# Two more products of the second block moved forward at each layer's start, in a three-layer fp32 transformer kernel

## What is computed

```
mod = silu(c) @ ada_w[i] + ada_b[i];  shift, scale, gate = split(mod, 3)
h   = rms_norm(x, norm_g[i]) * (1 + scale) + shift
proj = h @ w_in                       # the stage that the change touches
out = mixer(proj) @ w_out             # retention, banded attention, latent attention
x   = x + gate * out
```

## Time and profile before

| | us |
|---|---|
| time, median of 3 runs | 2511.5 (2510.46 to 2511.74) |
| the profiled execution, its own time | 2513.0 |
| its span, first to last instruction | 2511.1 |
| TensorE busy | 2455.8 |
| VectorE busy | 1620.3 |
| GpSimd busy | 1221.9 |
| ScalarE busy | 1111.1 |

### The profile page before, as it was taken

How to read it: one execution, slowest core, us unless ns; L and a number is a source line. 1 busy time by engine, 2 the same in 40 slices (tenths; PEclk the granted TensorE clock), 3 DMA queues, 4 the chain that set the end, 5 groups by cost and what they waited for, 6 DMA issues and landing times.

```text
span 2511.1 us, 38631 instructions
## 1 busy us (share of the span) xinstructions
PE 2455.8 (98%) x15068; PEld 2154.1 (86%) x15068; DVE 1620.3 (65%) x2189; ACT 1111.1 (44%) x2060; POOL 1221.9 (49%) x873
## 2 busy tenths in 40 slices
PE   6999999999999999999999999999999999899999
PEld 5888898865588899999998899999988888688887
DVE  6966656487533399795876335666434679888864
ACT  4322223334444342222223336777534434788861
POOL 1545545430044455554455445565454455566664
PEclk9999999999999999999999999999999999999999
DMA  6454544484034334442333357454134353200034
GB/s 261 147 177 140 191 143 165 153 312 138 27 109 157 110 132 151 165 147 93 110 109 118 109 156 208 133 156 117 61 122 159 105 171 98 91 1 1 1 119 158
DMA packets 239472, 327.89 MB, mean 131 GB/s; under 512 B 19246, under 2 KB 172078, under 8 KB 237500
## 3 DMA queue, kind: packets, MB, share of 16 engines
q1 hardware_dynamic: 237820, 325.32, 39.1%
q10 hardware_dynamic: 1472, 0.10, 0.0%
HBM read 246.06 MB, written 79.33 MB: 130 GB/s over the span
## 4 chain that ended last, share of the span: by engine, by line
PE 87%; DVE 8%; issue 2%; ACT 1%; DMA 1%; SPq 0%; POOL 0%; DVEq 0%; ACTq 0%
PE ps L1042 22%; PE ps L1044 22%; PE ps L1043 22%; PE ps L1345 4%; PE ps L1485 2%; PE ps L1333 2%; PE ps L1467 2%; PE ps L1261 2%; PE ps L1280 2%; DVE s_raw L2056 1%; PE ps L1274 1%; PE ps L1185 1%; DVE s_lo L2043 1%; PE ps L1056 1%; DVE raw L2073 1%
## 5 line engine op out<-in xcount | busy, mean ns | idle before, releaser
L932 POOL TENSOR_TENSOR w_lo<-raw,w_hi 128x512 fp32r<-128x512 f32 (+1 forms) x570 | 825.6, 1456 | 1006.7 <-ACT w_hi L1567 1006.0
L1567 ACT ACTIVATE w_hi<-raw 128x512 fp32r<-128x512 f32 (+1 forms) x574 | 355.4, 628 | 1008.5 <-PE ps L1044 796.7
L1042 PE MATMUL ps<-w_hi,s_hi 128*128 128x256 f32 (+1 forms) x1088 | 308.6, 284 | 1.6 <-DVE s_lo L2043 1.3
L1043 PE MATMUL ps<-w_lo,s_hi 128*128 128x256 f32 (+1 forms) x1088 | 307.3, 282 | 0.0
L1044 PE MATMUL ps<-w_hi,s_lo 128*128 128x256 f32 (+1 forms) x1088 | 307.3, 282 | 0.0
L2087 DVE TENSOR_TENSOR u<-u,ps 128x1024 f32<-128x1024 f32 (+1 forms) x128 | 155.3, 1213 | 184.6 <-PE ps L1044 180.2
L1042 PE MATMUL ps<-w_hi,a_hi 128*128 128x256 f32 (+1 forms) x816 | 230.6, 283 | 0.0
L1043 PE MATMUL ps<-w_lo,a_hi 128*128 128x256 f32 (+1 forms) x816 | 230.5, 283 | 0.0
L1044 PE MATMUL ps<-w_hi,a_lo 128*128 128x256 f32 (+1 forms) x816 | 230.5, 282 | 0.0
L2073 DVE TENSOR_TENSOR raw<-raw 128x1024 f32<-128x1024 f32 (+1 forms) x128 | 179.6, 1403 | 60.1 <-DMA raw<-in_w 57.2
L1042 PEld LDWEIGHTS ps<-w_hi,s_hi 128*128 128x128 f32 x1088 | 208.7, 192 | 9.9 <-issue 9.4
(11 more groups left out here) (320 smaller groups left out, 5966.3 us busy)
## 6 DMA issues: line engine op xcount, KB each, us to landing
raw<-in_w SPq DMA_DIRECT2D x191, 512.0 KB, 4.5
ada_c<-in_ada SPq DMA_DIRECT2D x14, 2304.0 KB, 10.4
blk<-u SPq DMA_DIRECT2D x62, 512.0 KB, 3.2
blk<-c SPq DMA_DIRECT2D x31, 512.0 KB, 3.9
blk<-m1s SPq DMA_DIRECT2D x31, 512.0 KB, 3.3
ada_first<-in_ada SPq DMA_DIRECT2D x12, 768.0 KB, 16.3
r_g<-blk SPq DMA_DIRECT2D x8, 1024.0 KB, 9.7
r_v<-blk SPq DMA_DIRECT2D x4, 2048.0 KB, 12.8
```

What stands on the lines that cost most here:

```text
L932: pool.tensor_tensor(w_ring(w_lo, n), w_source(n), w_ring(w_hi, n).bitcast(F32), ALU.subtract)\
L1042: pe.matmul(out, a_hi_, b_hi_, start=first, stop=False, skip_group_check=True)
L1043: pe.matmul(out, a_hi_, b_lo_, start=False, stop=False, skip_group_check=True)
L1567: act.activation(w_ring(w_hi, n), w_source(n), ACT.Copy).then_inc(w_rounded, 1)
```

## The change

Product 0 of the second block moves from third to second place, and product 1 from behind the whole first block to fourth place. Products 0 and 1 of the second block are accumulated in one pair of PSUM banks: ScalarE copies product 0 out (now to a tile of its own, `m1_second`), then product 1 is added on top by TensorE, and `evict(s, "c11")` becomes a copy. Product 1 gets its own weights tile and load. The transposes stay in the second product of the order. The order of VectorE's fourth weight sum in the first block, the bank numbers and the waits on them follow.

```diff
-    start = [(first, 0), (first, 1), second[0]] + [(first, i) for i in range(2, 7)] + second[1:]
+    start = [(first, 0), second[0], (first, 1), second[1]] + [(first, i) for i in range(2, 7)] + second[2:]
...
-        raw_second = place("raw_second", 124, [P, 1024])
+        raw_second = [place(f"raw_second{i}", at, [P, 1024]) for i, at in enumerate((124, 120))]
+        m1_second = [place(f"m1_second{l}", at, [P, 1024]) for l, at in enumerate((186, 186, 196))]
...
             if s in FIRST_BLOCK[0:3]:
-                return (0, 1, 2, 3, 1, 3, 2)[i]
+                return (0, 0, 2, 3, 0, 3, 2)[i]
             if s - 1 in FIRST_BLOCK[0:3]:
-                return (0, 1, 0, 2, 3, 1, 2)[i]
+                return (1, 1, 1, 3, 0, 2, 3)[i]
...
             load_raw(R11, 0)
+            load_second(0, 0)
             load_raw(R21, 0)
...
-            load_second(0)
+            load_second(0, 1)
...
-                        if s == FIRST_BLOCK[l] and i == 1 and k == 1:
+                        if (s, i, k) == (FIRST_BLOCK[l] + 1, 0, 1):
                             turn_half(l, 1, range(4, 8))
...
             def m1s_copy(s):
                 act.wait_ge(w_used, product_end(s, 0))
-                act.wait_ge(stored["c21"], 16 * s)
-                act.activation(quad_tile(m1s, s), product_banks(s, 0), ACT.Copy).then_inc(m1s_done, 1)
+                if s - 1 not in FIRST_BLOCK[0:3]:
+                    act.wait_ge(stored["c21"], 16 * s)
+                act.activation(quad_tile(m1_home(s), s), product_banks(s, 0), ACT.Copy).then_inc(m1s_done, 1)
...
-                hi(PRODUCT[s, 1])
+                hi(PRODUCT[s + 1, 0])
                 if l:
                     stats(l, 1, 3)
-                hi(PRODUCT[s, 1] + 1)
+                hi(PRODUCT[s + 1, 0] + 1)
                 m1s_copy(s)
-                product_slots(s + 1, 0)
+                product_slots(s, 1)
...
-                product_slots(s + 1, 1)
+                product_slots(s + 1, SECOND_ORDER[2])
...
+                if what == "c11" and s - 1 in FIRST_BLOCK[0:3]:
+                    dve.tensor_copy(quad_tile(c11, s), product_banks(s, 1)).then_inc(ev, 1)
+                    return
...
-                for n in range(2 if l else 0, 4):
+                for n in range(2 if l else 0, 3):
                     weight_sum(s, n)
                 variant_low(l, "a22", 0)
                 turned(l, 1, 1)
+                weight_sum(s, 3)
                 variant_low(l, "a22", 1)
                 evict(s, "c11")
```

More of the change, by code:

```diff
@@ L273, in build_program @@
         ld = [sem(f"raw_in{j}") for j in range(5)]
-        second_in = sem("second_in")
+        second_in = [sem(f"second_in{i}") for i in range(2)]
         w_rounded, w_split, w_used = sem("w_rounded"), sem("w_split"), sem("w_used")
@@ L408, in raw_quad, with second_quad, m1_home @@
             return raw[j][:, 0:4 * BLOCKS[s][3]].rearrange("p (k n) -> p k n", k=4)
-        def second_quad(s):
-            return raw_second[:, 0:4 * BLOCKS[s][3]].rearrange("p (k n) -> p k n", k=4)
+        def second_quad(s, i):
+            return raw_second[i][:, 0:4 * BLOCKS[s][3]].rearrange("p (k n) -> p k n", k=4)
+        def m1_home(s):
+            return m1_second[FIRST_BLOCK.index(s - 1)] if s - 1 in FIRST_BLOCK[0:3] else m1s
         def ada_bank(s):
@@ L422, in w_source @@
                 nw = BLOCKS[s][3]
-                if i == 0 and s - 1 in FIRST_BLOCK[0:3]:
-                    return second_quad(s)[:, 2 * j:2 * j + 2]
+                if i < 2 and s - 1 in FIRST_BLOCK[0:3]:
+                    return second_quad(s, i)[:, 2 * j:2 * j + 2]
                 return raw_quad(SOURCE[i], s)[:, 2 * j:2 * j + 2]
@@ L570, in load_raw, with load_second @@
                     .then_inc(ld[j], 16)
-            def load_second(l):
+            def load_second(l, i):
                 s = FIRST_BLOCK[l] + 1
@@ L576, in load_second @@
                     sp.wait_ge(w_used, out_end(l - 1, 3))
-                nw, w0 = BLOCKS[s][3], BLOCKS[s][0]
-                sp.dma_start(second_quad(s), t["w"][w0:w0 + 4, :, 0:nw].rearrange("k p n -> p k n")).then_inc(second_in, 16)
+                nw, w0 = BLOCKS[s][3], BLOCKS[s][0] + 4 * i
+                sp.dma_start(second_quad(s, i), t["w"][w0:w0 + 4, :, 0:nw].rearrange("k p n -> p k n"))\
+                    .then_inc(second_in[i], 16)
             def load_pair(l, p):
@@ L727, in out_loads @@
                 if l < LAST:
-                    load_second(l + 1)
+                    for i in range(2):
+                        load_second(l + 1, i)
                     for b in range(4):
@@ L1064, in bank_wait @@
                         pe.wait_ge(ev, evicted(s - 1, "c12"))
-                    if i < 2 and s > 0:
+                    if i == 0 and s > 0:
                         pe.wait_ge(o_free, 16 * FIRST_BLOCK.index(s) - 4)
+                    if i == 1:
+                        pe.wait_ge(m1s_done, s + 1)
                     if i > 3:
@@ L1070, in bank_wait @@
                 if s - 1 in FIRST_BLOCK[0:3]:
[L1071 to L1076, removed]
+                    if i == 1:
+                        pe.wait_ge(m1s_done, s + 1)
+                    elif i in (3, 4, 5):
+                        pe.wait_ge(ev, evicted(s - 1, {3: "v", 4: "u3", 5: "c12"}[i]))
+                    elif i in (2, 6):
+                        pe.wait_ge(ev, evicted(s, {2: "c11", 6: "u2"}[i]))
                     return
                 if s - 2 in FIRST_BLOCK[0:3] and i < 4:
-                    pe.wait_ge(ev, evicted(s - 1, ("c21", "v", "c12", "u3")[i]))
-                    if i == 3 and s - 1 in ADA_BLOCKS:
+                    pe.wait_ge(ev, evicted(s - 1, ("u3", "c21", "v", "c12")[i]))
+                    if i == 0 and s - 1 in ADA_BLOCKS:
                         pe.wait_ge(m_row, ADA_BLOCKS.index(s - 1) + 1)
@@ L1095, in block_product @@
                 out = product_banks(s, i)
+                added = i == 1 and s - 1 in FIRST_BLOCK[0:3]
                 bank_wait(s, i)
@@ L1104, in block_product @@
                         k = 2 * j + e
-                        if s == FIRST_BLOCK[l] and i == 1 and k == 1:
+                        if (s, i, k) == (FIRST_BLOCK[l] + 1, 0, 1):
                             turn_half(l, 1, range(4, 8))
-                        if s == FIRST_BLOCK[l] and i == 1 and k == 3:
+                        if (s, i, k) == (FIRST_BLOCK[l] + 1, 0, 3):
                             turn_half(l, 1, range(4))
@@ L1114, in block_product @@
                                 mm = product(out[:, b], hi[:, e, cut], lo[:, e, cut], x_hi[v][:, k], x_lo[v][:, k],
-                                             k == 0, k == 3)
+                                             k == 0 and not added, k == 3)
                             else:
                                 mm = product(out[:, b // 2, b % 2], x_hi[v][:, k, cut], x_lo[v][:, k, cut],
-                                             hi[:, e], lo[:, e], k == 0 and b % 2 == 0, k == 3)
+                                             hi[:, e], lo[:, e], k == 0 and b % 2 == 0 and not added, k == 3)
                     mm.then_inc(w_used, 1)
@@ L1546, in hi @@
                     _, s, i, j = kind
-                    if i == 0 and s - 1 in FIRST_BLOCK[0:3]:
+                    if i < 2 and s - 1 in FIRST_BLOCK[0:3]:
                         if j == 0:
-                            act.wait_ge(second_in, 16 * (FIRST_BLOCK.index(s - 1) + 1))
+                            act.wait_ge(second_in[i], 16 * (FIRST_BLOCK.index(s - 1) + 1))
                     elif j == 0 and i in (0, 1, 6):
@@ L1668, in first_block @@
                     turned(l, 1, k)
-                hi(PRODUCT[s, 2])
+                m1s_copy(s + 1)
+                hi(PRODUCT[s + 1, 1])
                 variant(l, "a22", 1)
                 turned(l, 1, 0)
-                hi(PRODUCT[s, 2] + 1)
+                hi(PRODUCT[s + 1, 1] + 1)
                 for k in (2, 3):
                     turned(l, 1, k)
+                product_slots(s, 2)
                 product_slots(s, 3)
@@ L1690, in projections @@
                                 product_slots(s, i + 1)
-                            elif i:
+                            elif i > 1:
                                 product_slots(s, SECOND_ORDER[i + 1])
@@ L1697, in projections @@
                                 hi(UP[n])
-                        if i == 1:
+                        if i == 1 and s > first:
                             m1s_copy(s)
@@ L2071, in weight_sum @@
                 if n == 3:
+                    if s - 1 in FIRST_BLOCK[0:3]:
+                        dve.wait_ge(ld[R21], 16 * raw_load(R21, s))
                     dve.wait_ge(w_split, product_end(s, 1))
@@ L2081, in evict @@
                 dve.wait_ge(w_used, product_end(s, i))
+                if what == "u2" and s in FIRST_BLOCK[0:3]:
+                    dve.wait_ge(w_split, product_end(s + 1, 1))
+                if what == "u2":
```

(1 more changed line is left out.)

## The result

The changed kernel takes **2531.5 us** (median of 4 runs, 2531.04 to 2533.48) against 2511.6 for the kernel before: the ratio is 1.0081, with a 95% interval from 1.0069 to 1.0093. It is 0.8% slower; 2532 was forecast. The profiled execution took 2533.5 us.

A forecast was written before the change was run, and what follows sets the result against it. TensorE, busy 98% of the span, was taken to bound the kernel. Starts 1.4, first-block end 14.4 and clock 4.8 sum to 20.6 us, so 2532 against a median of 2511.5; range 2528 to 2537, with most rivals 2520 to 2538.

The forecast's parts named there:

- Term 1: Starts of the three layers: VectorE's sums get more time but its chain starts later; -1.1, +1.4, +1.1, together +1.4 us.
- Term 2: End of the first block: TensorE waits at x+1.4 for the weight-sum chain, 5.0, 5.0 and 4.4, sum 14.4 us.
- Term 3: Behind the three waits at x+1.4 TensorE's clock falls to half rate, costing 1.6 us each, 4.8 us.
- rival (a): Behind the new waits at x+1.4 the clock doesn't fall; 2527 us, chance 0.12.
- Taken at nothing: Items counted as free: c11 copy, ScalarE's m1 copy, second-block bank waits, the extra 512 KB load, u2's wait for GpSimd.

The follow-up runs named there:

- sums_early: The changed kernel with the second block's first two weight sums ahead of the evictions of c22 and v on VectorE; 2512.8 us, ratio 1.0008 to the kernel before.
- c11_behind_sums: The changed kernel with two weight sums early and the c11 eviction moved behind the first four operand sums on VectorE; 2511.6 us, ratio 1.0000.
- wait_filled: The changed kernel with 20 extra matmuls ahead of x+1.4 in each layer, into the banks it then overwrites; 2526.6 us, ratio 1.0059.
- before_s2_first: The kernel before, with ScalarE's rounding of the first half of s2 ahead of the two weight slots of 0.3; 2511.1 us, ratio 0.9998.
- c11_second: The changed kernel with the order 0.0, 0.1, 1.0, 1.1 at each start, banks, transposes and loads to match; 2546.5 us, ratio 1.0144.
- c11_second_sums_early: The changed kernel with the order 0.0, 0.1, 1.0, 1.1 at each start and the two weight sums early; 2528.9 us, ratio 1.0069.
- one_sum_ahead: The changed kernel with only the weight sum that 1.4 reads moved just ahead of the eviction of c12; 2517.4 us, ratio 1.0025.

## Why the prediction was right

Read from the two profiles, in us. A start is the time from 0.0 to the end of 0.6, less the product that was moved in; the clock's share is what 1.4 and the products behind it take longer than in the kernel before.

| | layer 0 | layer 1 | layer 2 | sum | predicted |
|---|---|---|---|---|---|
| starts | -1.3 | +0.6 | +0.1 | -0.6 | +1.4 |
| wait at x+1.4 | 5.1 | 5.1 | 4.5 | 14.7 | 14.4 |
| clock | 2.0 | 2.8 | 1.7 | 6.4 | 4.8 |

The sum is 20.5, where 20.6 was predicted; the medians differ by 20.0. That it fits so closely is luck: term 1 was 2.0 too high and terms 2 and 3 were 1.9 too low. The waits are counted from the end of the last matmul's turn; the brackets in the rows count from the end of its longer record and show 4.92, 4.93 and 4.33.

**Term 2** was right in place, length and cause. The waits are within 0.1 of those worked out from the earlier trace rows. sums_early shows the cause: with the sum ahead of the eviction of c12 they go.

**Term 1** had the right mechanism and came out 2 us too high, with the wrong sign: the starts were forecast to lose 1.4 us and gained 0.6. In layer 0 the c11 eviction starts at 71.23 (71.7 predicted) and VectorE's chain to u2 takes 24.04 (24.2 predicted, 22.9 before). In layers 1 and 2 it takes 24.03 and 23.96, so GpSimd's tiles add only 0.3 to 0.4 to the 23.7 and 23.6 of the earlier trace rows, and the eviction comes 0.7 and 0.8 us earlier than worked out. The new wait of 0.8 at 13.0, with which the prediction reckoned, isn't there. ScalarE is released by the load 3.6 us after the issue, not 4.2, and GpSimd's first tile ends at 886.27, when 12.0 ends as well:

```profile
880.65 0.92 SPq L582 DMA_DIRECT2D raw_second<-in_w  x2
...
884.98 1.29 POOL L939 TENSOR_TENSOR w_lo<-raw_second,w_hi 128x512 fp32r<-128x512 f32 x1 [7.76 <-ACT w_hi L1577]
```

The Trainium skill ("SBUF — State Buffer", Who interferes with whom) has VectorE and GpSimd lock each other out of their port pair. c11_behind_sums agrees: a sum under a GpSimd tile took 2.3 us against 1.2. But by the full price of two tiles the chain of layer 0 would have been 25 us, and it was 24.0: a tile costs the chain less where VectorE has an idle stretch to take a part of it, as the first sum of c11_behind_sums suggests. No run isolates this.

**Term 3** was right in mechanism and undersized, 4.8 against 6.4. The term took the half-rate stretch behind a 2 us wait for that behind one of 5 us: 3.3 us there, and 4.3, 6.2 and 3.2 here. wait_filled shows that this is the clock and not contention. The Trainium skill ("TensorE: Matmul & The Clock Gate", Part 1: The HAM clock gate) says that half of the throttled time is lost; half of 4.3, 6.2 and 3.2 is 6.9, and the rows give 6.4.

The row on which this term and the case against rival (a) rest was itself the exception, and one trace could not show that. The same wait in the changed kernel's latent attention left the clock at 1.00:

```profile
2421.71 1.17 PE L1477 MATMUL ps<-ident,l_p 128*128 128x128 f32 x8 [1.99 <-DVE l_pT L2707]
```

Each of the twelve profiles has a wait of 1.97 to 2.02 us at this place, and the clock fell behind it in two of them (before and before_s2_first). The forecast that it falls behind all three waits of 4.3 to 4.9 us held, but this row was weaker ground for it than it looked.

**Taken at nothing**: nothing in the runs speaks against it for the changed kernel. But ScalarE's copy of 1.0, one of those items, held up two engines in c11_second, where its product stood one place later, and that run was 15 us slower than the changed kernel. The item was safe only for the order that the change chose.

The profiled span is longer by 20.4, not 20.5: -0.4 ahead of 0.0, +2.1 in retention (below), and -1.8 in latent attention, where waits for l_p shift from one execution to the next and the wait above left the clock up. What makes them shift wasn't tried.

## What to carry to other kernels

When a product is taken away from a place, ask what chain it had been covering, and follow that chain through every engine's queue: here the price of a good reordering was one weight sum that stood behind an eviction, 5 us three times, with the clock on top. In these runs a wait of 5 us on TensorE cost its length and about 2 us more, one of 1 to 1.7 us at x+1.4 its length, and between the two it went either way (below). When a freed wait doesn't turn into time, look for the next instruction that stands in a queue behind something later than its own input; three such places (VectorE's sums, ScalarE's copy, ScalarE's rounding of s2) had to be put right, with one more change of the order, between a loss of 0.8% and a gain of 0.3%.

## What was unexpected in the hardware

The clock fell in the changed kernel's profile at one more place, in retention, where the kernel before has the same work. TensorE waited 1.64 us for ScalarE and then 0.43 us for a DMA, and the four matmuls behind took 3.47 us against 1.96:

```profile
546.79 3.47 PE L1271 MATMUL ps<-r_v,r_kd 128*128 128x512 f32 x4 [0.43 <-DMA r_v<-blk]
...
547.00:548.00 1.00, 1.00 (x2) 0.54 1.04 381
548.00:549.00 1.00, 1.00 (x2) 0.50 1.06 389
```

In the kernel before, the same four matmuls after a wait of 1.66 alone, and then c11_second, where the second wait was longer still and the clock stayed up (its window has PE busy, PEclk, DMA share, GB/s):

```profile
541.03 1.96 PE L1261 MATMUL ps<-r_v,r_kd 128*128 128x512 f32 x4
```

```profile
549.12 1.10 PE L1269 MATMUL ps<-r_v,r_kd 128*128 128x512 f32 x2 [0.66 <-DMA r_v<-blk]
...
550.00:551.00 1.00, 1.00 (x4) 1.00 1.05 387
```

Of the twelve profiles, four have that second wait: with 0.43 and 0.50 (c11_behind_sums) the clock fell, with 0.15 and 0.66 it did not. Put together with the other waits of these runs:

| wait of TensorE | place | the clock fell |
|---|---|---|
| 4.3 to 4.9 us | x+1.4, changed kernel and c11_second | 6 of 6 |
| 2.6 to 3.1 us | x+1.1, c11_second and c11_second_sums_early | 5 of 6 |
| 1.97 to 2.02 us | latent attention, all twelve profiles | 2 of 12 |
| 1.6 to 1.7 us, then 0.15 to 0.66 us | retention | 2 of 4 |
| 1.6 to 1.7 us alone | retention | 0 of 8 |
| 1.1 to 1.7 us | x+1.4, one_sum_ahead | 0 of 3 |

In c11_second the 3.07 us wait of layer 0 (before 72.18) left the clock at 1.00 and the equal one of layer 1 (before 905.38) lowered it. So a longer wait lowers it more often, but the length alone doesn't tell. What else decides it these runs don't settle.
